# Moving four large tiles to the front of SBUF and dropping a padding tile

## The reference

```
x = x + 0.5 * post1(SwiGLU_1(pre1(x)))        # D_FF = 2816
u = pre_m(x);  P = u @ w_in                   # 3328 columns
    P -> windowed attention (|i-j| <= 128, 8 heads, 2 kv heads, rotary, sink)
       | HGRN2: gated linear recurrence in both directions, 4 heads of 128
x = x + post_m(concat(RMSNorm(attn), HGRN2_out) @ w_out)
x = x + 0.5 * post2(SwiGLU_2(pre2(x)))

swiglu(x) = (silu(x @ w_gate) * (x @ w_up)) @ w_down
```

## The kernel before

| tile | start | remainder by 2048 |
|---|---|---|
| `vec_rows`, `vecs`, `sink`, `HGN`, `small`, `ident`, `ones`, `eps`, `rt_root`, `rt` | 16,512 to 19,648 | various |
| `row_pad` (832 bytes, never read or written) | 19,648 | 1216 |
| `xT` | 20,480 | 0 |
| `raw`, `WH`, `WL` (16,384 each) | 36,864, 53,248, 69,632 | 0 |
| `RSB`, `TMP`, `SQ`, `SQX`, `SS`, `SSX` | 86,016 on | 0 |
| `XH`, `XL` (with `YB` at the place of `XL`) | 104,448, 120,832 | 0 |
| `hh`, `xin`, `xout`, `V`, `YM` (one region, used in turn) | 137,216 | 0 |
| `hl` | 182,272 | 0 |

## Time and profile before

### The profile page before, as it was taken

How to read it: one execution, slowest core, us unless ns; L and a number is a source line. 1 busy time by engine, 2 the same in 40 slices (tenths; PEclk the granted TensorE clock), 3 DMA queues, 4 the chain that set the end, 5 groups by cost and what they waited for, 6 DMA issues and landing times.

```text
span 1187.0 us, 13314 instructions
## 1 busy us (share of the span) xinstructions
PE 1091.4 (92%) x4943; PEld 885.7 (75%) x4943; DVE 585.5 (49%) x773; ACT 336.3 (28%) x486; POOL 458.0 (39%) x211
## 2 busy tenths in 40 slices
PE   3999999999999789898899789878999999999996
PEld 2788888888888568677677356757888888888884
DVE  5485544552000666686773653656655545510004
ACT  4322222222222343232224533333222222222211
POOL 3454444444444453131221500445444444444420
PEclk8999999999999799999899779979999999999996
DMA  6043333323332322121211000221333333323301
GB/s 218 19 135 94 95 100 90 104 83 96 98 97 86 113 71 71 55 53 38 70 36 54 18 1 1 71 72 53 107 88 106 88 105 90 97 85 96 97 16 71
DMA packets 173627, 93.12 MB, mean 78 GB/s; under 512 B 11476, under 2 KB 169752, under 8 KB 173592
## 3 DMA queue, kind: packets, MB, share of 16 engines
q1 hardware_dynamic: 173168, 92.55, 26.2%
q10 hardware_dynamic: 424, 0.10, 0.0%
HBM read 90.54 MB, written 2.10 MB: 78 GB/s over the span
## 4 chain that ended last, share of the span: by engine, by line
PE 82%; DVE 10%; issue 3%; ACT 2%; POOL 1%; DMA 1%; SPq 0%; DVEq 0%; POOLq 0%; ACTq 0%
PE ps L634 23%; PE ps L635 23%; PE ps L636 23%; PE ps L875 2%; PE ps L768 2%; PE ps L731 1%; PE ps L805 1%; PE ps L732 1%; PE ps L733 1%; DVE xT L1001 1%; PE ps L890 1%; POOL SSX L357 1%; DVE TMP L1000 1%; DMA raw<-ffn_w_up 1%; DVE S L1265 1%
## 5 line engine op out<-in xcount | busy, mean ns | idle before, releaser
L344 POOL TENSOR_TENSOR WL<-raw,WH 128x1024 fp32r<-128x1024 f32 x168 | 404.6, 2411 | 658.3 <-ACT WH L405 658.3
L634 PE MATMUL ps<-XH,WH 128*128 128x512 f32 x912 | 365.6, 401 | 18.1 <-DVE XL L980 8.0
L635 PE MATMUL ps<-XL,WH 128*128 128x512 f32 x912 | 360.2, 395 | 0.0
L636 PE MATMUL ps<-XH,WL 128*128 128x512 f32 x912 | 359.7, 394 | 0.0
L405 ACT ACTIVATE WH<-raw 128x1024 fp32r<-128x1024 f32 (+1 forms) x170 | 176.0, 1038 | 542.9 <-PE ps L636 517.7
L634 PEld LDWEIGHTS ps<-XH,WH 128*128 128x128 f32 x912 | 174.8, 192 | 57.0 <-DVE XL L980 9.7
L636 PEld LDWEIGHTS ps<-XH,WL 128*128 128x128 f32 x912 | 174.3, 191 | 37.2
L635 PEld LDWEIGHTS ps<-XL,WH 128*128 128x128 f32 x912 | 174.6, 191 | 35.2
L634 PE MATMUL ps<-hh,WH 128*128 128x512 f32 x352 | 136.9, 389 | 0.0
L635 PE MATMUL ps<-hl,WH 128*128 128x512 f32 x352 | 136.9, 389 | 0.0
L636 PE MATMUL ps<-hh,WL 128*128 128x512 f32 x352 | 136.9, 389 | 0.0
(11 more groups left out here) (148 smaller groups left out, 977.4 us busy)
## 6 DMA issues: line engine op xcount, KB each, us to landing
raw<-ffn_w_gate SPq DMA_DIRECT2D x44, 512.0 KB, 3.7
raw<-ffn_w_up SPq DMA_DIRECT2D x44, 512.0 KB, 3.7
raw<-ffn_w_down SPq DMA_DIRECT2D x32, 448.0 KB, 3.2
raw<-w_in SPq DMA_DIRECT2D x22, 512.0 KB, 3.7
raw<-ffn_w_down SPq DMA_DIRECT2D x16, 512.0 KB, 3.4
raw<-w_out SPq DMA_DIRECT2D x8, 512.0 KB, 3.4
xin<-x SPq DMA_DIRECT2D x4, 512.0 KB, 5.1
raw<-w_in SPq DMA_DIRECT2D x8, 256.0 KB, 3.1
```

Source lines behind the costliest of these rows:

```text
L344: pool.tensor_tensor(WL[:, s, 0:size], raw[:, s, 0:size], WH[:, s, 0:size].bitcast(fp32), ALU.subtract).then_inc(lo_done, 3 if n == 2 else 1)
L634: nc.tensor.matmul(dst, WH[:, s, w], xh, start=first, stop=False)
L635: nc.tensor.matmul(dst, WH[:, s, w], xl, start=False, stop=False)
L636: return nc.tensor.matmul(dst, WL[:, s, w], xh, start=False, stop=last)
```

## The change

The four largest tiles used throughout are asked for first, ahead of the small ones, and the padding tile is gone. No instruction, wait or shape differs.

```diff
+        xT = sb("xT", [P, KD, TOK])
+        raw = sb("raw", [P, NSLOT, SLOT])
+        WH, WL = sb("WH", [P, NSLOT, SLOT], f32r), sb("WL", [P, NSLOT, SLOT], f32r)
         NV = 6 * KD + 4 * NH + 4
         vec_rows = sb("vec_rows", [NV, P])
         vecs = sb("vecs", [P, NV])
...
         ident = sb("ident", [P, P])
         ones, eps = sb("ones", [P, 1]), sb("eps", [P, 1])
         rt_root, rt = sb("rt_root", [P, 6, TT]), sb("rt", [P, 6, TT])
-
-        sb("row_pad", [P, 208])
-        xT = sb("xT", [P, KD, TOK])
-        raw = sb("raw", [P, NSLOT, SLOT])
-        WH, WL = sb("WH", [P, NSLOT, SLOT], f32r), sb("WL", [P, NSLOT, SLOT], f32r)
         RSB = sb("RSB", [P, TOK])
```

## The result

The changed kernel takes 1196.15 us at the median of 6 runs (1191.78 to 1198.66), the kernel before 1183.58 (1182.35 to 1188.83). The ratio on record is 1.0097, 95% interval 1.0074 to 1.0119; that of these two medians is 1.0106. The kernel is slower by 1%, outside the range of 1180 to 1193 that was forecast. The profiled execution of the changed kernel took 1197.23 us, with a span of 1195.3 and a mean granted clock of 0.945; that of before took 1188.83, with 1187.0 and 0.949.

The account below looks back on a forecast made before the run. The prediction took TensorE, busy at the full clock with one matmul each 0.226 us, to bound the kernel. All four terms were 0, so it forecast the earlier kernel's median, 1185.7 us, with a range of 1180 to 1193.

Parts of the forecast that it names:

- term 1: TensorE's 3792 large matmuls at 0.226 us: shifted operands cost 0 to 2.5 ns each, at most 9.5 us; taken as 0.
- TensorE pays: Rival: each large matmul pays for operands straddling a 2048-byte boundary, up to +9.5 us, so 1195; chance 0.10.
- TensorE gains: Rival: operands both starting on multiples of 2048 collided, so matmuls get faster, up to 49 us, to 1137; chance 0.06.
- Term 2: VectorE, ScalarE and GpSimd instructions: no change with address, at most 1.8 us on VectorE and 0.2 on GpSimd; taken as 0.
- Term 3: Steady-state weight loads: 3.7 us each, some 12 us between landing and use, so even a quarter slower stays hidden; zero.
- Term 4: First loads and last store: up to a quarter slower at unaligned addresses, together 0 to 2.2 us; taken as 0.
- the start falls in another order: Rival: at the start VectorE's short products finish before GpSimd's read holds them up, up to -4.2 us, so 1181.5; chance 0.05.
- The three cases within 0.5%: Whole kernel: no effect (0.74), slower loads (0.05), other order at the start (0.05), all within 5.9 us.

Follow-up runs that it names:

- after_plus_192: The changed kernel with 192 bytes of padding between the small tiles and RSB; 1182.93 us against 1184.59 for the kernel before, ratio 0.9992.
- moving_off: The kernel before with 1216 bytes of padding behind WL, shifting RSB, XH, XL, hh, hl but not the weights; 1213.3 us against 1184.29, ratio 1.024.
- pad_removed: The kernel before without its padding tile, the order of tiles as it was; 1183.74 us against 1185.96, ratio 0.9981.
- all_32: The kernel before with 32 bytes more padding ahead of xT, so every large tile shifts alike; 1183.72 us against 1185.0, ratio 0.9996.
- sweep_224_1024_1088: The kernel before with moving operands 224 (gate and up), 1024 (FFN 1 down) and 1088 bytes (FFN 2 down) past a multiple of 2048; 1209.53 us, one run.
- order_only: The changed kernel with the padding tile back in front of RSB, so only the new order remains; 1209.02 us, ratio 1.0192 to the kernel before.
- one_tile_a: The kernel before with one tile per FFN stage shifted, by 256: XL at 192, FFN 1's hh at 192, FFN 2's hl at 64; 1201.59 us, one run.

## Why the prediction was wrong

**The step that failed** is term 1, the matmuls: "I take 0". Its upper bound held for this layout: 2.5 ns for each from the earlier trace rows, and 2.22 were measured, 3792 x 2.22 = 8.4 us. I took the lower end because the tree levels on TensorE did not follow their offsets. They were a poor stand-in. They have 128 columns and mostly start 0.112 us apart, twice a quarter of 0.2267, so their columns don't set their pace and 2 ns could hide; that is argued, no run tests it. That they still take 0.91 and 0.89 us after the change says nothing, because both their operands (`W` and `KM`) lie behind RSB and moved alike. The rival "TensorE pays" had a chance of 0.10 and a price of 9.5. Its loss is what happened, though not by the straddle that it named, and `after_plus_192` shows that the whole 12.6 us come with the distance. That 2.5 ns lay so near 2.22 is luck: it came from a rounding of 0.02 us in eight other matmuls, and as a bound for any layout it was too low, since `moving_off` lost 6.7 a matmul.

**Its mechanism was wrong as well, in the rival too.** I had the straddle of a stretch of 2048 as what could cost. In `pad_removed` and `all_32` each operand straddles one, and nothing is lost; in `sweep_224_1024_1088` an operand at 1024 straddles too, and nothing is lost. What the change does is to move two groups of tiles by different amounts, 3,968 and 832 bytes. I had written both remainders down and compared each with 2048. The one place where I compared them with each other was the rival "TensorE gains". There I wrote that the weights of block k lie 512 bytes further for each k and that the intervals don't alternate. That was an observation in favour of a period that divides 512, and I read it as one against any effect.

**TensorE gains** did not occur: distance 0 is the cheapest found. The 13 ns between 226.67 and half of the 427 at the lower clock are still unexplained.

**Term 2**, the other engines: right, 0.68 us for the level products in both kernels.

**Term 3**, the loads in the steady state: right, though its own figures give 21.8 - 3.7 - 3.5 = 14.6 us between landing and use, not 12. A unit's landing went from 3.7 to 3.8 us (gate) and 3.9 (up) and stayed hidden. As before, ScalarE waited for loads only at the start, twice for a gate unit, 6.6 us against 6.2, and twice for an up unit, 1.3 against 0.9:

```profile
ACT WH L403 <- DMA raw<-ffn_w_gate: 6.6, 2, 5.9
```

**Term 4**, the ends: I took 0 and kept up to 0.38 us a unit. It was 0.29 and 0.27 for the first two, 1.81 / 1.52 = 1.19. The section "How a descriptor splits into AXI transactions" of the Trainium skill's "DMA: Bandwidth & Descriptors", which speaks of where reads start, would make it 20 / 16 = 1.25, an estimate; the trace agrees in kind. Each kernel whose `raw` was off a multiple of 256 had its first splits 1.8 us apart, `all_32` among them, and each with `raw` on one had 1.5. The same delay gave more back: the rival **the start falls in another order** came in as well, for half of its price, 1.9 us by the end of the first stage against 4.2.

**The sum.** In the profiled executions the terms are +8.4 for the matmuls, about +1.0 for the 192 with swapped roles (5.2 ns each), -1.9 at the start, and +0.8 that remain, for 8.3. The medians are 12.6 apart. All executions on record close most of that gap. Of the changed kernel there are 25; one took 1235.44 us at a mean clock of 0.873 and is left out here. Of the other 24, five took 1191.8 to 1192.6 us and nineteen 1195.1 to 1204.2. Of the kernel before there are 78: 65 took 1182.2 to 1186.5 us and thirteen 1188.8 to 1190.7. The medians of the shorter groups are 7.3 us apart (1191.9 and 1184.6), those of the longer ones 7.2 (1196.5 and 1189.4), which is what the terms give without the 0.8: 7.5. The rest of the difference is that the changed kernel was in its longer group in 19 of 24 cases, against 13 of 78; over all of them the medians are 1196.3 and 1184.7, 11.6 apart.

Two traces at distance 0 show what sets such groups apart there. `all_32` was profiled with a span of 1181.9 us at a mean clock of 0.956, `after_plus_192` with 1186.0 at 0.949. From 785 to 830 us, in the first units of FFN 2, 5 of the large matmuls of the one and 20 of the other stood 0.427 us apart, at half the clock, and 15 x 0.2 = 3.0 of the 4.1 us lie there. Both profiled executions of the comparison, 1188.83 and 1197.23, belong to the longer groups. Why the changed kernel falls into its longer group so often no run shows; `after_plus_192`, with the same order and distance 0, had three of its ten executions there (1187.9 to 1189.0 us).

**The chances**: slower had 0.11. The three cases within 0.5%, 0.84 together, all rested on one belief, that addresses don't matter to TensorE, and that belief on one row of another kind of matmul. It bore far less weight than 0.84.

## What to carry to other kernels

When tiles move in SBUF, compare the moves with each other before comparing any with a boundary: here all large tiles could move by 32 or 832 bytes for nothing, while two groups that moved differently cost 1% to 2.4%. For matmuls like these (fp32r operands, 512 columns, TensorE busy at the full clock), give the tiles that stream through TensorE and those that are loaded as its weights, high and low parts alike, the same remainder by 256 bytes, and check it by the distance between starts of consecutive matmuls at the full clock, which shows 2 ns where the busy share shows nothing. A small difference at the start can flip the order of two engines, so read the start of a trace separately before blaming a layout for it.

## What the hardware showed that I had not expected

- At the full clock 128x512 matmuls of fp32r operands started 226.67 ns apart when all four tiles had one remainder by 256, and 228.89, 231.11, 231.99, 232.39, 233.33, 234.28 or 234.44 otherwise. 233.33 is 6.67 above the first, and 228.89 is a third of that above it. In the FFN stages of the changed kernel the three products of a triple differ: 229.2, 231.6 and 225.8 ns to the next start, and elsewhere in that run the three values change places.
- At half the clock the distance was 0.427 us in every layout looked at, `moving_off`, `order_only` and `one_tile_a` included.
- The Trainium skill, "SBUF — State Buffer", section "Who interferes with whom", says that TensorE and ScalarE never wait on anyone, and "TensorE: Matmul & The Clock Gate", section "Step-by-step: what each phase is for", that loading the next weights takes no read bandwidth from the running matmul. The runs sit badly with the second: the distance between the weights' place and the moving operand's decides whether a matmul takes 226.67 ns or more (228.89 after the change). That it is these two reads that meet is my guess and was not shown.
- The same layout can run at two paces: `order_only` at 232.4 ns in FFN 1 and 233.3 in FFN 2, both at distance 128.
